# Delta rule with transposes in place of products, stick-breaking suffix sums in two single-pass products, and gates spread over the group

## The reference

```python
z = q @ k.T * scale                         # causal: s < t
log_1mb = where(causal, log_sigmoid(-z), 0)
suffix = cumsum(log_1mb, reverse) - log_1mb
a = where(causal, exp(log_sigmoid(z) + suffix), 0);  out = a @ v
```

## Time and profile before

| | |
|---|---|
| median of three runs | 2819.57 us |
| profiled execution, its own time | 2821.64 us |
| its span | 2819.9 us |
| TensorE busy / weight loads busy | 96% / 82% |
| VectorE / ScalarE / GpSimd busy | 66% / 42% / 20% |
| mean granted TensorE clock | 0.984 |
| stick-breaking stage, its first to its last TensorE work | about 18 to 292 us |
| delta-rule stage | about 295 to 679 us |

### The profile page before, as it was taken

One profiled execution on the slowest core, in us unless ns is written; L12 is line 12 of the kernel. 1 busy time (PEld: TensorE's weight loads), 2 busy tenths in 40 slices (PEclk: granted clock), 3 DMA queues, 4 the chain that ended last, 5 costly groups with the idle time before them and its releaser, 6 DMA issues.

```text
span 2819.9 us, 36339 instructions
## 1 busy us (share of the span) xinstructions
PE 2701.4 (96%) x13797; PEld 2314.1 (82%) x13797; DVE 1858.7 (66%) x3485; ACT 1175.5 (42%) x1893; POOL 562.8 (20%) x426
## 2 busy tenths in 40 slices
PE   8999999989999999999998999999999999999997
PEld 6777888878877899999998888888888746788886
DVE  3335656655555677876995888888888575544434
ACT  5544342342222545445997233333333355422322
POOL 0122220220000577875000111111111024000000
PEclk9999999999999999999999999999999999999999
DMA  4111201002653478775667988998996211222230
GB/s 165 53 53 67 83 31 45 31 4 107 226 205 138 159 281 293 280 270 178 257 247 273 354 324 331 349 347 310 348 343 249 98 47 59 82 105 90 90 105 30
DMA packets 141214, 501.15 MB, mean 178 GB/s; under 512 B 13257, under 2 KB 66929, under 8 KB 111473
## 3 DMA queue, kind: packets, MB, share of 16 engines
q1 hardware_dynamic: 122608, 364.60, 36.3%
q0 software_dynamic: 18432, 134.23, 12.1%
HBM read 450.53 MB, written 48.25 MB: 177 GB/s over the span
## 4 chain that ended last, share of the span: by engine, by line
PE 81%; DVE 8%; ACT 4%; DMA 3%; issue 2%; POOL 1%; SPq 0%; ACTq 0%; DVEq 0%; POOLq 0%
PE bank L247 21%; PE bank L249 21%; PE bank L248 21%; PE bank L2157 2%; DVE xn L1534 2%; PE bank L1119 1%; PE bank L1125 1%; DMA w_raw<-in_w_in_dram 1%; PE bank L1109 1%; PE bank L742 1%; PE bank L2640 1%; PE bank L349 1%; ACT whl L237 1%; DVE whl L243 1%; PE bank L2747 1%
## 5 line engine op out<-in xcount | busy, mean ns | idle before, releaser
L247 PE MATMUL bank<-HH,uhl 128*128 128x384 f32 x1024 | 345.7, 338 | 1.9 <-POOL uhl L1660 1.9
L249 PE MATMUL bank<-HH,uhl 128*128 128x384 f32 x1024 | 342.8, 335 | 0.0
L248 PE MATMUL bank<-HL,uhl 128*128 128x384 f32 x1024 | 342.6, 335 | 0.0
L247 PE MATMUL bank<-vhl,awhl 128*128 128x512 f32 x768 | 301.2, 392 | 10.2 <-DVE awhl L2374 9.2
L1716 POOL DMA_INDIRECT gs<-in_uv_dram,idx x128 | 152.6, 1193 | 770.0 <-DVE x L1741 477.6
L248 PE MATMUL bank<-vhl,awhl 128*128 128x512 f32 x768 | 300.6, 391 | 0.0
L249 PE MATMUL bank<-vhl,awhl 128*128 128x512 f32 x768 | 300.5, 391 | 0.0
L2314 ACT ACTIVATE vhl<-vraw 128x1024 fp32r<-128x1024 f32 x128 | 135.7, 1061 | 320.1 <-PE bank L249 283.6
L1660 POOL TENSOR_TENSOR uhl<-ur,uhl 128x1024 fp32r<-128x1024 f32 x69 | 168.1, 2448 | 319.9 <-ACT uhl L1654 319.6
L243 DVE TENSOR_TENSOR whl<-w_raw,whl 128x2048 fp32r<-128x2048 f32 x49 | 114.1, 2328 | 159.8 <-ACT whl L237 159.8
L247 PE MATMUL bank<-HH,whl 128*128 128x512 f32 x528 | 213.1, 404 | 3.4 <-DVE whl L243 3.4
(11 more groups left out here) (428 smaller groups left out, 6157.8 us busy)
## 6 DMA issues: line engine op xcount, KB each, us to landing
ur<-in_peer_u_dram SPq DMA_DIRECT2D x128, 512.0 KB, 5.1
vraw<-in_peer_v_dram SPq DMA_DIRECT2D x128, 512.0 KB, 6.3
w_raw<-in_w_in_dram SPq DMA_DIRECT2D x36, 1024.0 KB, 5.0
xn<-in_ada_rows_dram SPq DMA_DIRECT2D x48, 512.0 KB, 4.5
g_scratch<-stg SPq DMA_DIRECT2D x12, 2048.0 KB, 8.1
gti<-g_scratch SPq DMA_DIRECT2D x16, 1536.0 KB, 12.0
wf_raw<-in_f_w_in_dram SPq DMA_DIRECT2D x22, 1024.0 KB, 4.8
act_scratch<-ag SPq DMA_DIRECT2D x96, 192.0 KB, 2.9
```

The source lines that it names most:

```text
L247: e.matmul(out, l[0], r[0], start=start, stop=False)
L248: e.matmul(out, l[0], r[1], start=False, stop=False)
L249: return e.matmul(out, l[1], r[0], start=False, stop=stop)
```

## The change

Stick-breaking: `Ls` is split into a rounded half `Lhi` and a rest `Llo`, both fp32r, by two VectorE instructions in segment 3, and each of the ten fp32 products becomes two fp32r products with an fp32r constant. `Lhi` takes the memory of `es`, `Llo` that of `Ls`. The sum L797 moves from segment 2 to segment 1. The constants `tri_ge` and `ones` are rounded in place once, at the start.

Delta rule: P^T X^T and the second subtraction go. In their place X is transposed on TensorE right behind P, and ScalarE copies it to XT. The last level now has all three steps (P, transposes, P^T X^T). GpSimd no longer builds XT. The silus move from segment 11 to segments 6 to 11, and the sums for the norms, their roots and what follows from them move to later segments.

```diff
-    cst = new.sb("cst", [P, len(CONSTS), P])
+    new.sb("before_cst", [P, 24])
+    with ExitStack() as ph:
+        cst = new.sb("cst", [P, len(CONSTS), P], scope=ph)
+    cst_r = new.sb("cst_r", [P, len(CONSTS), P], F32R)
+    exact = lambda n: cst_r[:, CI[n], :]
...
# pe_sb_head, seg 4
-            e.wait_ge(*G.of("L", pair, hh, NT - 1))
+            e.wait_ge(*V.of("lo", pair, hh))
...
-                    i = e.matmul(b[:, (j - s) * P:wid[s]], const("tri_ge") if j == s else ones,
-                                 L[:, off[j]:off[j] + wid[j]], start=j == s, stop=j == NT - 1,
-                                 skip_group_check=True)
+                    for part in (Lhi[hh], Llo[hh]):
+                        i = e.matmul(b[:, (j - s) * P:wid[s]], exact("tri_ge" if j == s else "ones"),
+                                     part[:, off[j]:off[j] + wid[j]], start=j == s and part is Lhi[hh],
+                                     stop=j == NT - 1 and part is Llo[hh], skip_group_check=True)
# dve_sb_head
-        if seg == 2:
-            ... the sum L797 ...
+        if seg == 3:
+            e.wait_ge(*G.of("L", pair, hh, NT - 1))
+            e.tensor_copy(Lhi[hh][:, :], L[:, :]).then_inc(*V.up("hi", pair, hh))
+            e.wait_ge(*V.of("hi", pair, hh))
+            e.tensor_tensor(Llo[hh][:, :], L[:, :], r32(Lhi[hh][:, :]), ALU.subtract).then_inc(*V.up("lo", pair, hh))
# dve_sb, behind both heads of segment 1
+                if seg == 1:
+                    dve_sb_sum(e, pair, 0)
+                    dve_sb_sum(e, pair, 1)
# pe_gdn_head, odd segments 3 to 13, behind P
+                b = R3.take("xt", h, l)
...
+                    i = e.transpose(b[:, blk(tb)], B["X"][:, tb, :], ident)
# even segments 4 to 14
-                ... X P (not at the last level) and P^T X^T ...
+                e.wait_ge(*A.of("xt", h, l))
+                e.wait_ge(*V.of("p", h, l))
...
+                    if l < LV - 1:
+                        i = e.matmul(b[:, blk(tb)], B["XT"][:, tb, :], PMs[f][:, tb, :], start=True, stop=True)
+                    else:
+                        i = e.matmul(b[:, blk(tb)], PMs[f][:, tb, :], B["XT"][:, tb, :], start=True, stop=True)
# act_gdn_head, odd segments 3 to 13
+            e.wait_ge(*T.of("xt", h, l))
+            e.activation(B["XT"][:, :, :], in4(R3.bank("xt", h, l)), ACT.Copy).then_inc(*R3.out(A, "xt", h, l))
# dve_gdn_head, even segments: one subtraction, from X (from XT at the last level)
# pool_gdn_head: L1283 and L1285 removed
+    SILU = {6: (0, 1), 7: (2,), 8: (3,), 9: (4,), 10: (5,), 11: (6, 7)}
# pe_gdn / act_gdn: sums and roots of the norms
-    seg in (12, 15)
+    seg in (14, 18)
# act_gdn: second squares 14 -> 16; dve_gdn: normed 13, 17 -> 15, 20
```

More of the change, by code:

```diff
@@ L620, in build @@
         zs = [new.sb(f"zs{i}", [P, 1280]) for i in range(2)]
-        Ls = [new.sb(f"Ls{i}", [P, 1280]) for i in range(2)]
-        es = [new.sb(f"es{i}", [P, 1280]) for i in range(2)]
+        with ExitStack() as ph2:
+            Ls = [new.sb(f"Ls{i}", [P, 1280], scope=ph2) for i in range(2)]
+            es = [new.sb(f"es{i}", [P, 1280], scope=ph2) for i in range(2)]
+        Llo = [new.sb(f"Llo{i}", [P, 1280], F32R) for i in range(2)]
+        Lhi = [new.sb(f"Lhi{i}", [P, 1280], F32R) for i in range(2)]
         wba = new.sb("wba", [P, KT, 16])
@@ L804, in dve_sb_head, with dve_sb_sum @@
                                 ALU.subtract).then_inc(*R2.out(V, "pre", pair, hh, s))
+    def dve_sb_sum(e, pair, hh):
+        T, A, V, G = SB
+        Z, L = zs[hh], Ls[hh]
+        e.wait_ge(*A.of("ln", pair, hh))
+        e.scalar_tensor_tensor(out=L[:, :], in0=Z[:, :], scalar=0.0, in1=L[:, :], op0=ALU.max,
+                               op1=ALU.add).then_inc(*V.up("l", pair, hh))
     def pool_sb_head(e, pair, hh, seg):
@@ L989, in dve_sb @@
             e.memset(cin[f][:, 0:3], 0.0).then_inc(*V.up("zero", f))
+        e.wait_ge(*c_land.of("c"))
+        i = CI["tri_ge"]
+        e.tensor_copy(cst_r[:, i:i + 2, :], cst[:, i:i + 2, :]).then_inc(*SB[2].up("exact"))
         for seg in range(6):
@@ L1110, in pe_gdn_head @@
                 i.then_inc(*T.up("p", h, l))
[L1111 to L1120, removed]
                 b = R3.take("xt", h, l)
@@ L1124, in pe_gdn_head @@
                 for tb in range(NT):
-                    i = e.matmul(b[:, blk(tb)], PMs[f][:, tb, :], B["XT"][:, tb, :], start=True, stop=True)
+                    i = e.transpose(b[:, blk(tb)], B["X"][:, tb, :], ident)
                 i.then_inc(*T.up("xt", h, l))
+            else:
+                e.wait_ge(*A.of("xt", h, l))
+                e.wait_ge(*V.of("p", h, l))
+                b = R3.take("x", h, l)
+                for s in R3.empty("x", h, l):
+                    e.wait_ge(*s)
+                for tb in range(NT):
+                    if l < LV - 1:
+                        i = e.matmul(b[:, blk(tb)], B["XT"][:, tb, :], PMs[f][:, tb, :], start=True, stop=True)
+                    else:
+                        i = e.matmul(b[:, blk(tb)], PMs[f][:, tb, :], B["XT"][:, tb, :], start=True, stop=True)
+                i.then_inc(*T.up("x", h, l))
         if seg == 15:
@@ L1180, in act_gdn_head @@
             e.activation(B["LT"][:, :, :], in4(R3.bank("lt", h)), ACT.Copy).then_inc(*R3.out(A, "lt", h))
+        if 3 <= seg < 3 + 2 * LV and seg % 2:
+            l = (seg - 3) // 2
+            if l == 0 and h >= 2:
+                e.wait_ge(*V.of("onw", h - 2))
+            e.wait_ge(*T.of("xt", h, l))
+            e.activation(B["XT"][:, :, :], in4(R3.bank("xt", h, l)), ACT.Copy).then_inc(*R3.out(A, "xt", h, l))
         if seg == 15:
@@ L1231, in dve_gdn_head @@
             else:
[L1232 to L1238, removed]
+                X = B["X"] if l < LV - 1 else B["XT"]
+                e.wait_ge(*T.of("x", h, l))
+                e.tensor_tensor(X[:, :, :], X[:, :, :], in4(R3.bank("x", h, l)),
+                                ALU.subtract).then_inc(*R3.out(V, "x", h, l))
         if 16 <= seg < 24:
@@ L1304, in pe_gdn @@
                         pe_gdn_norm(e, 2 * g - 2 + f)
-                    if g < 3 and seg in (12, 15):
-                        pe_gdn_ones(e, R3, g + 1, (2 if seg == 15 else 0) + f)
+                    if g < 3 and seg in (14, 18):
+                        pe_gdn_ones(e, R3, g + 1, (2 if seg == 18 else 0) + f)
                     if g < 3 and seg == 16:
@@ L1325, in act_gdn @@
                         act_gdn_proj(e, R3, g + 1, STEP[seg])
-                    if seg == 11:
[L1327 to L1331, removed]
+                    if seg == 6 and g == 0:
+                        for i in (6, 7):
+                            act_gdn_silu(e, 0, i)
+                    for i in SILU.get(seg, ()):
+                        act_gdn_silu(e, g + 1, i)
+                    if seg == 11:
                         for i in range(2):
@@ L1363, in dve_gdn @@
                     for f in range(2):
-                        if seg in (13, 17):
-                            dve_gdn_normed(e, g + 1, (2 if seg == 17 else 0) + f)
+                        if seg in (15, 20):
+                            dve_gdn_normed(e, g + 1, (2 if seg == 20 else 0) + f)
                         if seg == 18:
```

25 lines of the change are left out of this document (6 added, 19 removed).

## The result

| | before | after |
|---|---|---|
| median of 5 runs | 2819.97 us (2815.47 to 2821.26) | 2774.4 us (2768.33 to 2777.7) |
| ratio, 95% interval | | 0.9835 (0.9824 to 0.9846) |
| profiled execution, its own time / span | 2821.64 / 2819.9 us | 2777.7 / 2776.0 us |
| first product of the delta-rule stage | 294.7 us | 287.6 us |
| its last norm sum, from there | 384.5 us | 340.2 us |

The kernel is 45.6 us faster; 2775 was forecast. Of the spans' difference, 7.1 us come from the stage of stick-breaking and 44.3 us from the delta-rule stage; 7.4 us are lost again in code that is the same in both.

What follows compares the result with a forecast made beforehand. TensorE was taken as the bound, with 81% of the chain that ended last. 6.4 + 15 - 3.5 + 20.5 + 9.7 - 3 = 45.1 us off 2821.6 gave 2776.5, stated as 2775; range 2764 to 2794.

Steps and rivals of the forecast that it cites:

- Suffix sums: Stick-breaking stage: 3.1 us saved in each of pairs 0 to 2, 0.9 and 2.0 us lost, 6.4 us saved.
- 128-wide starts stand 0.11 us apart: Suffix sums L742: sign of being right that the 128-wide rows start 0.11 us apart on TensorE.
- Pair 0's loss of 0.9 us: Stick-breaking, pair 0: gate computations stand behind the split on VectorE, ScalarE waits, a bank is delayed by about 0.9 us.
- Levels: Delta rule, levels 1 to 4, 16 in all: transposes replace products, 0.92 us a level, 15 us saved.
- First levels: Delta rule, four first levels: 44.0 us become 23.5 as holes mostly close, 20.5 us saved.
- The 2 us of slow clock: Delta rule, first level of group 3: 2 us of slow clock with the remaining hole of 2.9 us.
- One mark: First levels: sign of being right that L541 on VectorE never takes 1.6 us in segment 2.
- Last levels and their holes: Delta rule: added transposes and a wait lose 3.5 us; last-level holes in groups 0 to 2 save 9.7 us.
- The waits for squares are gone: Delta rule, last levels: sign of being right that TensorE no longer waits for the squares, 4.9 us in three waits.
- Moved work: Delta rule: moved roots, squares, second sums and norms on ScalarE and VectorE, 3 us lost allowed, bounds -1 and 6.
- The slack of about 1 us: Delta rule: each moved piece of work has about 1 us of slack by the predicted order of the queues.
- Sum: Whole kernel: the terms add to 45.1 us saved, 2776.5 us, stated as 2775 for the median.

Runs made afterwards that it cites:

- e1: Kernel before with only the stick-breaking part, the suffix sums' split and the sum a segment earlier: 2810.76 us, ratio 0.9970.
- e8: The changed kernel itself, run again unaltered for a second profile: 2771.61 us, ratio 0.9835 to the kernel before.
- e2: Kernel before with only transposes for products and GpSimd no longer building XT; silus stay in segment 11: 2803.3 us, ratio 0.9932.
- e6: Changed kernel with both heads' splits ahead of VectorE's convolution and decays in the last pair: 2766.05 us, ratio 0.9819.
- e9: Changed kernel, last pair's decays between the two splits, head 0's sums read ahead of the third convolution: 2764.97 us, ratio 0.9814.
- e4: Changed kernel, but GpSimd still builds XT, which ScalarE's copy then overwrites: 2781.89 us, ratio 0.9863.
- e3: Kernel before with only the silus spread and the norms' sums, roots, squares and scalings moved: 2806.83 us, ratio 0.9952.
- e7: e6 with the delta-rule stage's second sums, roots, norms and VectorE's gating of the previous group placed later: 2766.33 us, ratio 0.9830.
- e10: e9 with e7's order in the delta-rule stage: 2761.95 us, ratio 0.9807.

## Why the prediction was right

By its own steps:

- **Suffix sums, 6.4 us forecast.** Pairs 0 to 2 save 3.1 us each, as forecast, and a head takes 2.76 us where 2.75 was worked out. The mark that 128-wide starts stand 0.11 us apart was too simple: they stand 0.06 and 0.12 apart, and the next product makes up the rest. Pair 0's loss of 0.9 us did not come. In the last pair the wait for `Llo` is 5.1 us (4 to 5 forecast) and the loss 3.05 us (2.0 forecast), in part because VectorE's splits were slow there, 1.80 us instead of 1.49. With 0.8 us from ahead of the stage, 7.1 us in the trace and 8.2 us in e1.
- **Levels, 15 us.** 0.94 us a level in group 3, and 1.05, 0.92 and 0.90 us for levels 1 to 3 of group 0, which have projections between them. 16 times 0.94 are 15.0 us.
- **First levels, 20.5 us.** They take 4.42, 4.69, 4.69 and 7.54 us, 21.3 instead of 44.0, so 22.7 saved. No hole of note is left in groups 0 to 2, and 2.65 us in group 3 (2.9 forecast). The 2 us of slow clock priced behind it did not come here or in e8, where the window shows 1.00, but 1.4 us of it came behind the same hole in e2, e6 and e9: the term was fair, and that it was nothing here is chance. That GpSimd beside VectorE has a part in the holes is shown by e4, for 7 to 8 us. One mark was wrong: one convolution instruction in each of groups 0 to 2 still takes 1.66 us, now beside GpSimd's scaling of q (3 such rows, before 9).
- **Last levels and their holes, -3.5 and 9.7 us.** The three stretches of the earlier trace rows take 22.6 us instead of 29.2, 6.6 saved, where the two terms give 7.1 for these groups (9.7 less three quarters of 3.5). "The waits for squares are gone" is right, and the first sums follow the last level without a wait.
- **Moved work, 3 us lost.** From L1133 to the next group's first product it is 15.7 us before and after. The slack of about 1 us was not there: the second sums wait 0.76 us for a bank that L590 reads, and L1175 waits 0.82 us for the state, in each of three groups (2.3 and 2.5 us in all). But 1.9 and 0.9 us of other waits are gone from the same place, and the allowance was not needed.
- **Sum.** Up to the end of the delta-rule stage the two profiles give 51.3 and 50.4 us, the medians 45.6 and 45.9. Against the stages, the forecast of 45.1 was low by the 3 us of moved work and 2 us of clock that did not come. That the medians meet it almost exactly is partly luck. The first profile loses 7.4 us again behind the stage, with 10.2 us more at 1.2 GHz there. The second profile was taken of an execution at the median of its kernel (2771.61 us), but the one profile of the kernel before, 2821.64 us, lies 4.2 us above that kernel's median on the second profile's chip. Its stage times may be long by up to that much, as e1's shorter delta with the same code says too.
- **What the prediction did not say:** that the parts need each other. Its terms for last-level holes and levels stand beside each other as if each could be had alone; e2 shows that the levels' gain is half given back while ScalarE's silus stay piled up.

## What to carry to other kernels

When work on the bounding engine gets shorter, ask what it will now arrive at sooner: here a pile of eight silus on another engine took back 11 us by waiting until it was spread. When an engine gets added work in a full stretch, list what each later instruction frees (a bank, a buffer) before choosing its place: with the same split the last pair lost 3 us in one order and gained 3 us in another, and the order that looked at only one of the two consumers gained nothing. Take a helper engine's work out from beside a critical one even if the helper has slack. And before a difference of a few us between two profiles is given a cause, compare the time that each spent at the lower clock.

## What the runs showed of the hardware

- Beside a GpSimd instruction with two inputs in SBUF, VectorE's instructions with two inputs in SBUF take about twice as long: 1.66 us for 0.75 (L544), 2.45 for 1.27 (two L1292). Beside GpSimd's one-input masks (L596, L598) L805 took 1.80 us for 1.49. There even the cast with one input (L803) took 1.25 instead of 0.82 us. Those that read PSUM did not change (L1256 1.27 in both). GpSimd is slowed too: in the last pair its masks took up to 1.88 us instead of 0.64.
- A pair of 128-wide fp32r products costs about 0.22 us, as much as the one fp32 product that it replaces. The split gains nothing at 128 columns; all of the gain is in the wider ones.
- Behind a hole of 5.14 us (last pair) the granted clock was 0.50, 1.2 GHz, for 5.2 us; behind one of 6.07 us (e2) 0.51 for 5.2 us; behind one of 2.65 us (group 3) it stayed at 1.00, 2.4 GHz, in the kernel after and in e8. Shorter holes have no fixed answer: behind the same hole of 2.65 us it fell in e2, e6 and e9, and behind the hole of 2.11 us ahead of the delta-rule stage, which all twelve profiles have, it fell in e3, e8 and e9 and in no other. Behind 1.44 us (e7, e10) it stayed. Windows of the kernel after for the hole of 5.14 us and for that of 2.65:

```profile
247.34:252.53 5.19, 5.19 (x21) 4.99 (x21) 5.05 (x6) 3.06 (x3) 1.62 (x2) 0.50 0.01 3
...
589.10:596.00 6.90, 6.90 (x58) 6.68 (x59) 4.06 (x7) 1.20 (x2) 0.00 (x0) 1.00 0.85 287
```
